# Second block: attention starts behind 7 projection steps, compressed branches last

## The chip, the cores and the metric

The kernel runs on one core of a Trainium2 chip, as one program. The metric is the device time of one execution in microseconds. TensorE (PE) does the matmuls, VectorE (DVE) and ScalarE (ACT) the elementwise work and everything that leaves PSUM, GpSimd (POOL) next to nothing here, and SyncE (SP) issues the loads. The engines run side by side; each works off its own list of instructions in order and waits on semaphores (counters) that the others raise.

## What is computed

A block of two layers (a mixture of experts among its parts) is followed by a second block of two layers, all in float32, on one sequence of 256 tokens of width 1024. The change is in the second block, in the part from the input projection to the mixers:

```python
for l in range(DEPTH):                                   # DEPTH = 2
    h = rms_norm_2(x, ln1_gain[l])
    proj = h @ w_in[l]                                   # 1024 x 2866, split into:
    (nsa_q, k_cmp, v_cmp, k_slc, v_slc, k_win, v_win, nsa_gate,
     mla_cq, mla_ckv, mla_kpe, ret_q, ret_k, ret_v, ret_gate) = jnp.split(proj, offsets, axis=-1)
    o_nsa = nsa_mixer(partial_rope(nsa_q), partial_rope(k_cmp), v_cmp, ...)   # 6 heads, 3 branches each
    o_mla = mla_mixer(mla_cq, mla_ckv, mla_kpe, ...)                          # 5 heads
    o_ret = retention_mixer(ret_q, ret_k, ret_v, ret_gate, ...)               # 5 heads
    x = x + jnp.concatenate([o_nsa, o_mla, o_ret], axis=-1) @ w_out[l]
    h = rms_norm_2(x, ln2_gain[l])
    x = x + jnp.square(jax.nn.relu(h @ w_up[l])) @ w_down[l]

# nsa_mixer, per head: gate0 * softmax(q @ kc) @ vc + gate1 * softmax(q @ k_slc) @ v_slc + gate2 * softmax(q @ k_win) @ v_win
# with kc = gelu(blocks(k_cmp) @ w1_k) @ w2_k, and vc likewise (15 compressed positions)
# mla_mixer: q and k come from the normalised latents: rms(c_q) @ w_uq, rms(c_kv) @ w_ukv, ropes on 32 of 96 dims
# retention_mixer: group norm of the retained values, times silu(ret_gate)
```

The selected and the window branch are both plain causal attention at this length. The three branches of a head are summed, so their order is free.

## The kernel before

One layer of the second block runs `block2_pe`, `block2_act` and `block2_dve` side by side, each engine its own function. The work between the norm and the retention is cut into *steps* and *units*, whose order is written out by hand in three tables and the list of branches.

**Steps.** `STEPS` is one list; a step is a projection (`p nq0`: 8 matmuls of 128 by 256 into a bank of `acc`, which ScalarE copies out), a rope (`r nq0`: one matmul that turns the halves, then three VectorE instructions, lines 930, 932, 935), a matmul from the latents (`m mq0`, `m mk0`, `m mv0`, line 3006, copied out by ScalarE in line 3027) or `sums` (the two sums of squares of the latents, lines 2923 to 2925). `p kpe` takes rq0 along and `p rk0` takes rg0. The steps alternate between two banks of PSUM: step n waits until what step n-2 left there is read (`step_read`), by ScalarE's copy for p and m, by VectorE's rope for r. `STEPS_FIRST` holds the 19 steps ahead of the attention; between them stand, in banks of their own, the three parts of the compression network: `cmp_hidden_pe` (line 2883), `cmp_join_pe` (line 2890, with GELU on ScalarE in 2867) and `cmp_out_pe` (lines 2898 and 2900).

**Units.** A unit u is one branch of one head. `att_pe`, `att_act` and `att_dve` go through units in pairs. On TensorE: the steps beside u (`BESIDE[u]`), at even u the scores of the next pair (line 1018) and the values of the last pair (lines 1048 to 1053), then the transposes ("turn") of unit u's probabilities (line 1028 for compressed, 1031 for the others). On VectorE: mask and maximum of unit u+1 (lines 1080, 1084), normalisation of unit u (1091 to 1104), at odd u the finished heads' outputs (line 1125), then the steps beside u. On ScalarE: exponentials of unit u+1 (line 1133), copies of the steps beside u (line 909 for projections), copy of the turned probabilities of u ("probT", line 1146 or 1148).

The units of before: for each of three head pairs the compressed, the selected and the window branch (units 0 to 17), then the five heads of the latent attention (units 18 to 22). Steps stand beside units 0 to 17; none stands beside the latent heads.

**ScalarE's tables.** A function of another table set needs a table load first. The exponential, the sigmoid of the gates (part of the nvw projections), GELU, the square root and the Silu of the gates rg0 to rg2 (applied when the projection is copied out) are such functions; copies and squares need none.

**Loads.** SP issues the loads in the order of the list `AFTER`, into a ring of 7 slots: the load of item n waits until the slot of item n-7 is freed, by the last matmul that reads it.

## Time and profile before

| | us |
|---|---|
| median of 3 runs | 2389.46 |
| lowest and highest run | 2384.75, 2391.63 |
| profiled execution: own time, its span | 2383.3 |
| attention part, layer 0 and layer 1 (norm's end to first retention scores) | 151.1, 149.6 |

The profiled execution has no time beside its span; what lies around it is not shown. A row of the timeline gives the start, the length and, in brackets, how long the engine was idle ahead of it and what ended that. Every float32 matmul stands as two passes, so 8 matmuls read x16.

### The profile page before, as it was taken

Reading aid. Unit: us, or ns where it says so; the run is one execution under the profiler, and the core shown is the slowest. Engines: PE = TensorE matmul, PEld = TensorE weight load, DVE = VectorE, ACT = ScalarE, POOL = GpSimd, SP = SyncE. Lnnn points to the kernel's source line nnn. Section 1 sums busy time; section 2 is a strip of 40 time slices with the busy share of each in tenths; the row PEclk is TensorE's granted clock in tenths of the full one; section 3 lists DMA queues with packets and bytes.
Section 4 is the critical chain, followed back from the end, with each engine's and each line's share of the span. In section 5 each row is a group of like instructions: output and inputs, shape, how many; then the busy total and the mean of one; then the engine's idle time right before and its main releaser. Section 6 shows DMA issues by size and latency. Waiting matters only on the chain.

```text
span 2383.3 us, 36172 instructions
## 1 busy us (share of the span) xinstructions
PE 2273.9 (95%) x15501; PEld 1593.8 (67%) x15502; DVE 916.8 (38%) x2168; ACT 391.0 (16%) x903; POOL 27.9 (1%) x52
## 2 busy tenths in 40 slices
PE   7989999998999999998999999889899999989999
PEld 5758998876763444434444444366589998659999
DVE  3664887448420000000000010034656733457763
ACT  3222100022320000000000000014520002451101
POOL 1010000000100000000000000000000000000000
PEclk8998999998899999999999999999999999999999
DMA  9471478933169999999989999982225463323541
GB/s 358 166 252 36 159 248 310 384 114 107 36 247 378 369 409 411 409 413 407 384 305 364 408 410 410 411 285 103 71 80 169 177 194 126 123 71 107 176 157 41
DMA packets 240082, 582.97 MB, mean 245 GB/s; under 512 B 22170, under 2 KB 106658, under 8 KB 227636
## 3 DMA queue, kind: packets, MB, share of 16 engines
q1 hardware_dynamic: 239348, 580.52, 65.6%
q8 instruction: 124, 2.03, 0.3%
q14 instruction: 34, 0.28, 0.0%
q0 software_dynamic: 576, 0.13, 0.0%
HBM read 579.58 MB, written 1.05 MB: 244 GB/s over the span
## 4 chain that ended last, share of the span: by engine, by line
PE 83%; DMA 6%; DVE 5%; SPq 2%; ACT 2%; issue 1%; DVEq 0%; ACTq 0%
PE wrk L2486 13%; PE acc L876 8%; PE acc L2546 5%; PE acc L3272 5%; PE acc L3304 5%; PE wrk L2471 4%; PE wrk L3304 4%; PE wrk L3272 4%; PE acc L1658 3%; DMA ring<-in_moe_w_down_dram 3%; PE acc L879 3%; PE wrk L2493 3%; PE wrk L1658 3%; PE acc L953 2%; PE acc L2529 2%; PE acc L968 2%
## 5 line engine op out<-in xcount | busy, mean ns | idle before, releaser
L2486 PE MATMUL wrk<-ring,hT 128*64 128x512 f32 (+1 forms) x1792 | 348.1, 542 | 6.7 <-DMA ring<-in_moe_w_up_dram 3.4
L2730 DVE TENSOR_TENSOR scratch<-scratch,wrk 128x512 f32<-128x512 f32 (+4 forms) x32 | 24.5, 767 | 802.3 <-PE wrk L2486 594.9
L2486 PEld LDWEIGHTS wrk<-ring,hT 128*64 128x64 f32 x1792 | 126.2, 137 | 203.9 <-issue 186.9
L876 PE MATMUL acc<-hT,ring 128*128 128x256 f32 x1024 | 232.5, 384 | 1.3 <-ACT scratch L909 0.5
L876 PEld LDWEIGHTS acc<-hT,ring 128*128 128x128 f32 x1024 | 194.0, 192 | 29.9 <-issue 1.9
L2546 PE MATMUL acc<-ring,scratch 128*64 128x512 f32 x784 | 177.7, 597 | 14.9 <-DMA ring<-in_moe_w_down_dram 14.9
L3349 DVE TENSOR_TENSOR ring<-ring 128x512 f32<-128x512 f32 (+1 forms) x192 | 155.2, 862 | 1.2
L2546 PEld LDWEIGHTS acc<-ring,scratch 128*64 128x64 f32 x784 | 54.0, 136 | 116.9 <-issue 102.2
L3304 PE MATMUL acc<-scratch,ring 128*128 128x128 f32 x1024 | 117.6, 275 | 0.0
L3304 PEld LDWEIGHTS acc<-scratch,ring 128*128 128x128 f32 x1024 | 116.0, 192 | 0.0
L2665 ACT ACTIVATE scratch<-wrk 128x512 f32<-128x512 f32 (+4 forms) x32 | 21.1, 661 | 527.2 <-PE wrk L2518 527.2
L2471 PE MATMUL wrk<-ring,hT 128*128 128x512 f32 x224 | 96.9, 593 | 0.0
L879 PE MATMUL acc<-ring,hT 128*128 128x384 f32 (+5 forms) x384 | 82.6, 372 | 10.4 <-ACT scratch L909 6.2
L3304 PE MATMUL wrk<-scratch,ring 128*128 128x128 f32 x768 | 89.0, 275 | 0.0
L3272 PE MATMUL acc<-mixT,ring 128*128 128x128 f32 x768 | 88.4, 275 | 0.0
L3304 PEld LDWEIGHTS wrk<-scratch,ring 128*128 128x128 f32 x768 | 87.4, 192 | 0.0
L3272 PEld LDWEIGHTS acc<-mixT,ring 128*128 128x128 f32 x768 | 87.0, 192 | 0.0
L909 ACT ACTIVATE scratch<-acc 128x256 f32<-128x256 f32 (+8 forms) x118 | 41.3, 360 | 259.5 <-PE acc L876 166.6
L879 PEld LDWEIGHTS acc<-ring,hT 128*128 128x128 f32 x384 | 61.1, 197 | 30.8 <-issue 7.3
L1678 PE MATMUL acc<-scratch,ring 128*128 128x256 f32 x352 | 78.7, 386 | 2.5 <-DMA ring<-in_ffn_w_down_dram 1.8
L2493 PE MATMUL wrk<-ring,hT 128*32 128x256 f32 (+1 forms) x1536 | 77.6, 354 | 0.0
L2471 PEld LDWEIGHTS wrk<-ring,hT 128*128 128x128 f32 x224 | 42.3, 190 | 52.5 <-issue 52.5
(459 smaller groups left out, 3002.9 us busy)
## 6 DMA issues: line engine op xcount, KB each, us to landing
ring<-in_moe_w_gate_dram SPq DMA_DIRECT2D x56, 2048.0 KB, 20.3
ring<-in_moe_w_up_dram SPq DMA_DIRECT2D x56, 2048.0 KB, 20.7
ring<-in_moe_w_down_dram SPq DMA_DIRECT2D x56, 2048.0 KB, 18.9
ring<-in_w_ada_dram SPq DMA_DIRECT2D x24, 2048.0 KB, 17.5
ring<-in_w_up_dram SPq DMA_DIRECT2D x32, 1024.0 KB, 6.6
ring<-in_w_down_dram SPq DMA_DIRECT2D x32, 1024.0 KB, 6.6
ring<-in_w_out_dram SPq DMA_DIRECT2D x8, 2048.0 KB, 9.0
ring<-in_w_in_dram SPq DMA_DIRECT2D x8, 1536.0 KB, 15.9
```

The lines of the kernel that those rows point to most:

```text
L876: mm = pe.matmul(acc[p0:p0 + m, bank, 0:S], cols(k), hT[:, k, :], start=(k == 0), stop=(k == KD - 1))
L879: mm = pe.matmul(acc[:, bank, 0:m], hT[:, k, t], cols(k), start=(k == 0), stop=(k == KD - 1))
L953: pe.matmul(accv[:, 4 * h + m, :], w[:, k, m * P:(m + 1) * P], mixT[:, k, :], start=(k == ks[0] and m % 2 == 0), stop=False, skip_group_ch ...
L1658: mm = pe.matmul(PRODUCT[x][:, t * P:(t + 1) * P], stationary[x][:, k, t * P:(t + 1) * P], moving[x][:, k, :], start=(k == 0), stop=(k == ...
L1678: mm = pe.matmul(accv[:, m, :], w[:, j, m * P:(m + 1) * P], DENSE_TILES[:, 4 * g + j, :], start=(g == 0 and j == 0 and m % 2 == 0), stop=( ...
L2471: mm = pe.matmul(flat_wrk[:, lo + c * 512:lo + (c + 1) * 512], hT[:, k, 0:P], w[:, at_, c * 512:(c + 1) * 512], start=(k == 0), stop=(k == ...
L2486: mm = pe.matmul(flat_wrk[h * HD:h * HD + HD, lo:lo + n2], hT[:, k, 0:HD], w[:, at_, h * n2:(h + 1) * n2], start=(k == 0), stop=(k == KD - ...
L2493: mm = pe.matmul(flat_wrk[quarter(c), lo + n2:lo + n2 + n4], hT[:, k, LIGHT:MIDDLE], w[:, at_, c * n4:(c + 1) * n4], start=(k == 0 and n2 ...
L2546: mm = pe.matmul(acc[h * HD:h * HD + HD, 0, :], turned[:, at_:at_ + HD], w[:, j, h * 512:(h + 1) * 512], start=(g == 0 and n == 0), stop=( ...
L3272: mm = pe.matmul(up_region(x)[:, t * P:(t + 1) * P], stationary[x][:, k, t * P:(t + 1) * P], moving[x][:, k, :], start=(k == 0), stop=(k = ...
L3304: mm = pe.matmul(PRODUCT[x][:, m * P:(m + 1) * P], stationary[x][:, t, m, :], moving[x][:, t, :], start=(i == 0 and t == 0 and m == 0), st ...
L3349: ins = dve.tensor_tensor(part(out_), part(a), part(b), ALU.subtract)
```

## The change

The order of steps and units is rewritten. Ahead of the attention stand 7 steps: nq0, nks, nvw0, rope nq0, nvw1, rope nks, nq1. The units run: selected branches of head pairs 0 and 1 (units 0 to 3), their window branches (4 to 7), selected and window branches of pair 2 (8 to 11), the compressed branches of all three pairs (12 to 17), then the latent heads (18 to 22). Steps stand beside units 0 to 21: beside 7 `c join` and kpe, beside 8 `c out`, rope kpe and `sums`, beside 9 rq1, beside 10 rq2 and rope rq0, beside 11 mq0 and rk1, beside 12 mq1, mq2 and rope rq1, beside 13 rk2, rope mq0 and mq3, beside 14 mq4, rope mq1, mk0 and mk1, beside 15 rope mq2, mk2, mk3 and rope rq2, beside 16 ropes mq3 and mq4, mk4, mv0 and mv1, beside 17 to 21 rk0, rv0, rv1, rg1 and rg2 with the ropes of rk1, rk2 and rk0 between. The compression network's three parts become steps (`c parts`, `c join`, `c out`) in the alternating banks, beside units 6, 7 and 8. Their intermediate tensors, the latent keys and the latent values get other places, since their old ones are in use then. The Silu of the gates moves from the copy of the projections to the start of the retention (`ret_act`). Each unit waits for its own inputs and no longer for those of the last. The load of the latents' weights moves ahead of three of the projection's. Heads of pair 2 share banks with those of pair 0, in other columns.

```diff
     for layer in range(DEPTH):
-        after += [("in2", layer, i) for i in range(3)] + [("cmp", layer)]
-        after += [("in2", layer, i) for i in range(3, len(IN2))] + [("mla", layer), ("decay", layer)] + [("out2", layer, h) for h in range(2)]
+        after += [("in2", layer, i) for i in range(3)] + [("cmp", layer), ("in2", layer, 3), ("mla", layer)]
+        after += [("in2", layer, i) for i in range(4, len(IN2))] + [("decay", layer)] + [("out2", layer, h) for h in range(2)]
         n = D_FF // 512
         for kind in ("sup", "sdown"):
...
@@ -1005,6 +1005,10 @@
 
             return ((0, 15), (16, 31)) if kind == "cmp" else ((0, P), (P, 384))
 
+        def head_sum(b):
+
+            return acc[b["p0"]:b["p0"] + HD, b["head"] % 2, b["col"]:b["col"] + S]
+
         def att_scores_pe(pe, tag, pair, branches):
             for u in pair:
                 for s, v in branches[u]["ready"]:
...
             plan += rk[1:] + rk[:1]
-            plan += rows("rv", 5, 0, 320, t_v) + heads5("rg", 6, 0, t_g, ACT.Silu)
+            plan += rows("rv", 5, 0, 320, t_v) + heads5("rg", 6, 0, t_g)
             return plan
 
         def rope2(l):
...
-        def cmp_gelu_act(act, l):
+        def cmp_parts_act(act, l, bank):
+            act.wait_ge(freed_by_pe, freeing(("cmp", l)))
+            act.activation(n_part, acc[:, bank, 0:2 * P].rearrange("p (a h) -> p a h", a=2), ACT.Copy)\
+               .then_inc(act_done, up("act", "hidden parts", l))
+
+        def cmp_gelu_act(act, l, bank):
             act.wait_ge(pe_done, at("pe", "hidden", l))
-            act.activation(n_hid[:, :, 0:30], wrk[:, 3, 0:64].rearrange("p (a n) -> p a n", a=2)[:, :, 0:30], ACT.Gelu_apprx_tanh)\
+            act.activation(n_hid[:, :, 0:30], acc[:, bank, 0:64].rearrange("p (a n) -> p a n", a=2)[:, :, 0:30], ACT.Gelu_apprx_tanh)\
                .then_inc(act_done, up("act", "hidden", l))
 
-        def cmp_act(act, l):
-            act.wait_ge(freed_by_pe, freeing(("cmp", l)))
-            act.activation(n_kcT[:, 0:15], wrk[:, 1, 0:15], ACT.Copy).then_inc(act_done, up("act"))
-            act.activation(n_vcT[0:15, :], wrk[0:15, 2, 0:P], ACT.Copy).then_inc(act_done, up("act", "compressed", l))
-
-        def cmp_hidden_pe(pe, l):
+        def cmp_act(act, l, bank):
+            act.wait_ge(pe_done, at("pe", "compressed", l))
...
-                act.activation(l_k[64:96, h, :], l_kpe[64:96, 0, :], ACT.Copy).then_inc(act_done, up("act", "kpe", l) if h == 4 else up("act"))
-
-
-
-
-        STEPS_FIRST = ("p nq0", "p nq1", "p nq2", "p nkc", "p nvc", "p nks", "r nkc", "p nvs0", "p nvs1", "r nks", "p nkw",
-                       "r nq0", "p nvw0", "r nq1", "p nvw1", "r nkw", "r nq2", "p cq0", "p cq1")
-        BESIDE = (("p ckv", "p kpe"), ("p rq1", "sums"), ("p rq2", "r kpe"), ("p rk1", "r rq0"), ("p rk2", "r rq1"),
-                  ("p rk0", "r rq2"), ("p rv0", "r rk1"), ("p rv1", "r rk0"), ("p rg1", "r rk2"), ("p rg2", "m mq0"),
-                  ("m mq1", "m mq2"), ("r mq0", "m mq3"), ("r mq1", "m mq4"), ("r mq2", "m mk0"), ("r mq3", "m mk1"),
-                  ("r mq4", "m mk2"), ("m mk3", "m mk4"), ("m mv0", "m mv1"))
...
+        BESIDE = (("r nq1", "p nkw"), ("r nkw", "p nvs0"), ("p nvs1", "p nkc"), ("r nkc", "p nq2"), ("r nq2", "p nvc"),
...
@@ -2978,6 +2989,8 @@
                 return act_done, at("act", "proj", ("2", l), BESIDE_IT.get(name, name))
             if kind == "m":
                 return act_done, at("act", "mla", l, name)
+            if kind == "c":
+                return act_done, at("act", {"parts": "hidden parts", "join": "hidden", "out": "compressed"}[name], l)
             if kind == "sums":
                 return dve_done, at("dve", "latent mean squares", l)
             return dve_done, at("dve", "rope", rope_step(l, name)[0], name)
...
             out = []
-            for i, br, g_ in [(i, br, g_) for i in range(3) for br in range(3) for g_ in range(2)]:
+            order = [(i, br) for half in ((0, 1), (2,)) for br in (1, 2) for i in half] + [(i, 0) for i in range(3)]
+            for i, br, g_ in [(i, br, g_) for i, br in order for g_ in range(2)]:
                 h, kind = 3 * g_ + i, ("cmp", "slc", "win")[br]
                 rows = slice(HD * g_, HD * g_ + HD)
...
                 out.append(dict(q=q, k=k, v=v, mask=K("cmp_hide") if br == 0 else K("causal"), kind="cmp" if br == 0 else "causal",
-                                scale=float(HD) ** -0.5, gate=lambda t, c=3 * h + br: n_gate[:, t, c:c + 1], first=br == 0,
-                                last=br == 2, head=2 * i + g_, p0=HD * (h % 2), place=mixT[HD * (h % 2):HD * (h % 2) + HD, h // 2, :],
-                                ready=[(act_done, at("act", "compressed", l)),
-                                       (dve_done, at("dve", "rope", ("2", l), "nq2"))] if (h, br) == (0, 0) else [],
+                                scale=float(HD) ** -0.5, gate=lambda t, c=3 * h + br: n_gate[:, t, c:c + 1], opens=br == 1 and i < 2,
+                                last=br == 0, head=2 * i + g_, p0=HD * (h % 2), col=S * (i // 2), over=[],
+                                place=mixT[HD * (h % 2):HD * (h % 2) + HD, h // 2, :],
+                                ready=[(act_done, at("act", "compressed", l)), (dve_done, at("dve", "rope", ("2", l), f"nq{i}")),
+                                       (dve_done, at("dve", "rope", ("2", l), ("nks", "nks", "nkw")[br]))][0 if br == 0 else 1:3 if br else 1],
+                                v_ready=[(act_done, at("act", "proj", ("2", l), ("nvs1", "nvs1", "nvw1")[br]))] if br else [],
                                 mask_ready=[]))
             for h in range(5):
                 p0 = HD * (h % 2)
-                out.append(dict(q=l_q[0:96, h, :], k=l_k[0:96, h, :], v=lambda t, h=h: l_v[:, t, HD * h:HD * h + HD],
-                                mask=K("causal"), kind="causal", scale=96.0 ** -0.5, gate=None, first=True, last=True, p0=p0, head=6 + h,
+                out.append(dict(q=l_q[0:96, h, :], k=l_k[h][0:96, :], v=lambda t, h=h: l_v[:, t, HD * h:HD * h + HD],
+                                mask=K("causal"), kind="causal", scale=96.0 ** -0.5, gate=None, opens=True, last=True, p0=p0, head=6 + h,
+                                col=0, over=((0, 4), (1, 5), (6,), (7,), (8,))[h],
                                 place=mixT[p0:p0 + HD, 3 + h // 2, :], mask_ready=[],
-                                ready=[(act_done, at("act", "mla", l, "mk4")), (dve_done, at("dve", "rope", ("mla", l), "mq4"))] if h == 0 else [],
+                                ready=[(act_done, at("act", "mla", l, f"mk{h}")), (dve_done, at("dve", "rope", ("mla", l), f"mq{h}"))],
                                 v_ready=[(act_done, at("act", "mla", l, "mv1"))] if h == 0 else []))
             return out
...
@@ -3130,6 +3151,9 @@
             outproj_first_pe(pe, items[1], 1, (0, 1), ATTENDED2)
 
         def ret_act(act, l):
+            act.wait_ge(act_done, at("act", "proj", ("2", l), "rg2"))
+            act.activation(t_g[UPPER, 0, :], t_g[UPPER, 0, :], ACT.Silu).then_inc(act_done, up("act"))
+            act.activation(t_g[:, 1:3, :], t_g[:, 1:3, :], ACT.Silu).then_inc(act_done, up("act", "ret gates", l))
             act.wait_ge(pe_done, at("pe", "ret out", l, 4))
             act.activation(t_q[UPPER, 0, :], acc[UPPER, 0, 0:S], ACT.Copy).then_inc(act_done, up("act"))
             act.activation(t_q[:, 1:3, :], acc[:, 1:3, 0:S], ACT.Copy).then_inc(act_done, up("act", "ret o", l))
...
 
-        LATENTS_AT, SHARED_KEY_AT = 0, 11
-        assert STEPS[-1] == "m mv1" and "p rg2" in STEPS[:steps_beside(SHARED_KEY_AT)[0]]
+        VALUE_BLOCKS_AT, KEY_BLOCKS_AT = 4, 3
+        LATENTS_AT, SHARED_KEY_AT = 7, 9
 
         def block2_pe(pe, l):
...
                 step_dve(dve, l, n)
-                if STEPS[n] == "r nkc":
-                    value_blocks_dve(dve, l)
-                if STEPS[n] == "r nkw":
-                    key_blocks_dve(dve, l)
 
             def beside(u):
                 if u == LATENTS_AT + 3:
                     latents_dve(dve, l)
                 for n in steps_beside(u):
                     step_dve(dve, l, n)
+                if u == VALUE_BLOCKS_AT:
+                    value_blocks_dve(dve, l)
+                if u == KEY_BLOCKS_AT + 2:
+                    key_blocks_dve(dve, l)
 
             att_dve(dve, tag, branches2(l), beside)
             ret_dve(dve, l)
```

What the order of the built program shows at three places, the names being as in the lines above.

ScalarE around the step that waits for the copies of the compressed keys and values. Before, the two copies (15 columns) stand ahead of the first unit:

```order
L2867 ACTIVATE scratch<-wrk 128x2x30
L909 ACTIVATE scratch<-acc 128x256
L2872 ACTIVATE scratch<-wrk 128x15
L2873 ACTIVATE scratch<-wrk 15x128
L1133 ACT_TABLE_LOAD
L1133 ACTIVATE scratch,stat<-scratch,stat 128x15 x4
L909 ACTIVATE scratch<-acc 128x256
L909 ACTIVATE scratch<-acc 32x256
L909 ACTIVATE scratch<-acc 64x256
L2929 ACTIVATE scratch<-scratch 128x512
```

After, they stand behind the squares of the latents (2939, 2940), a probT (1152), a load and the exponentials of unit 9:

```order
L2873 ACT_TABLE_LOAD
L2873 ACTIVATE scratch<-acc 128x2x30
L909 ACTIVATE scratch<-acc 32x256
L909 ACTIVATE scratch<-acc 64x256
L2939 ACTIVATE scratch<-scratch 128x512
L2940 ACTIVATE scratch<-scratch 128x256
L1152 ACTIVATE scratch<-wrk 128x384
L1137 ACT_TABLE_LOAD
L1137 ACTIVATE scratch,stat<-scratch,stat 128x128
L1137 ACTIVATE scratch,stat<-scratch,stat 128x256
L2878 ACTIVATE scratch<-acc 128x15
L2879 ACTIVATE scratch<-acc 15x128
```

So the copies (2878, 2879) moved behind two table loads, GELU's and the exponential's, and a unit; on TensorE the step `sums` (2933) follows two steps behind them.

TensorE in the latent steps (3006 before and 3021 after are latent matmuls, 921 ropes). Before, one rope stands in each unit:

```order
L921 MATMUL acc<-scratch,const 96x256
L3006 MATMUL acc<-scratch,ring 64x256
L1028 MATMUL wrk<-const,scratch 15x128 x2
L921 MATMUL acc<-scratch,const 96x256
L3006 MATMUL acc<-scratch,ring 64x256
L1018 MATMUL wrk<-scratch 128x128 x2
L1018 MATMUL wrk<-scratch 128x256 x2
L1048 MATMUL acc<-scratch 64x256 x2
L1031 MATMUL wrk<-const,scratch 128x128 x3
L921 MATMUL acc<-scratch,const 96x256
L3006 MATMUL acc<-scratch,ring 64x256
```

After, units 14 to 16 carry two ropes and two to three latent matmuls with hardly anything between:

```order
L921 MATMUL acc<-scratch,const 96x256
L3021 MATMUL acc<-scratch,ring 64x256 x2
L1022 MATMUL wrk<-scratch 128x15 x4
L1052 MATMUL acc<-scratch 64x256 x2
L1032 MATMUL wrk<-const,scratch 15x128 x2
L921 MATMUL acc<-scratch,const 96x256
L3021 MATMUL acc<-scratch,ring 64x256 x2
L921 MATMUL acc<-scratch,const 128x256
L1032 MATMUL wrk<-const,scratch 15x128 x2
L921 MATMUL acc<-scratch,const 96x256 x2
L3021 MATMUL acc<-scratch,ring 64x256
L3021 MATMUL acc<-ring,scratch 128x320 x2
```

What moved is that the latent matmuls and their ropes stand beside six units instead of nine, all of compressed branches.

TensorE in the latent heads. Before, only scores, values and turns are there:

```order
L1018 MATMUL wrk<-hT,scratch 128x128 x2
L1018 MATMUL wrk<-hT,scratch 128x256 x2
L1031 MATMUL wrk<-const,scratch 128x128 x3
L1018 MATMUL wrk<-hT,scratch 128x128 x2
L1018 MATMUL wrk<-hT,scratch 128x256 x2
L1051 MATMUL acc<-scratch 64x256 x2
L1053 MATMUL acc<-scratch 64x128 x2
L1031 MATMUL wrk<-const,scratch 128x128 x6
```

After, projections (876, 879) and the last ropes stand between them:

```order
L1022 MATMUL wrk<-table,scratch 128x128 x2
L1022 MATMUL wrk<-table,scratch 128x256 x2
L1052 MATMUL acc<-scratch 64x256 x2
L1035 MATMUL wrk<-const,scratch 128x128 x3
L879 MATMUL acc<-ring,hT 128x320 x8
L921 MATMUL acc<-scratch,const 128x256
L1035 MATMUL wrk<-const,scratch 128x128 x3
L876 MATMUL acc<-hT,ring 128x256 x8
L921 MATMUL acc<-scratch,const 64x256
L1022 MATMUL wrk<-mixT,scratch 128x128
L1022 MATMUL wrk<-mixT,scratch 128x256
L1055 MATMUL acc<-scratch 64x256 x2
```

The retention's own projections moved here from beside units 5 to 9.

## Rows read from the trace of the kernel before

**Rows 1.** The page: the chain that ended last, share of the span by engine.
```profile
PE 83%; DMA 6%; DVE 5%; SPq 2%; ACT 2%; issue 1%; DVEq 0%; ACTq 0%
```

**Rows 2.** Busy time by stretch: length; PE, PEld, DVE, ACT, POOL; granted clock; DMA.
```profile
1600.00:1628.40 28.40, 25.02 (x201) 20.84 (x200) 10.01 (x28) 9.13 (x25) 0.00 (x0) 1.00 0.10 32
1628.40:1700.00 71.60, 70.30 (x380) 47.40 (x380) 36.56 (x169) 36.84 (x98) 0.00 (x0) 1.00 0.38 132
1700.00:1713.40 13.40, 10.39 (x63) 5.76 (x62) 10.82 (x49) 8.18 (x32) 0.00 (x0) 1.00 0.01 2
1713.40:1730.30 16.90, 11.63 (x67) 7.60 (x66) 10.74 (x50) 7.71 (x28) 0.00 (x0) 0.90 0.00 0
2099.60:2113.00 13.40, 10.26 (x63) 5.63 (x62) 10.92 (x49) 8.29 (x32) 0.00 (x0) 1.00 0.01 2
2113.00:2128.40 15.40, 10.25 (x68) 6.73 (x67) 10.58 (x50) 7.71 (x28) 0.00 (x0) 1.00 0.00 1
```

**Rows 3.** Timeline of TensorE in the head: start, length, operation, idle before.
```profile
1611.19 0.59 PE L921 MATMUL acc<-scratch,const 128*128 128x256 f32 x2
1613.61 2.25 PE L879 MATMUL acc<-ring,hT 128*128 128x146 f32 x16 [1.82 <-ACT scratch L909]
```

**Rows 4.** Timeline of ScalarE at the same place.
```profile
1612.07 1.28 ACT L909 ACT_TABLE_LOAD   x1
```

**Rows 5.** Timeline of TensorE: pair kpe+rq0; a projection to the next projection.
```profile
1632.60 9.07 PE L892 MATMUL acc<-hT,ring 128*32 128x256 f32 x32
...
1658.07 3.62 PE L876 MATMUL acc<-hT,ring 128*128 128x256 f32 x16
...
1663.89 0.44 PE L892 MATMUL acc<-hT,ring 128*64 128x256 f32 x2
```

**Rows 6.** Timeline of ScalarE: squares of the latents; probT, table load, two exponentials.
```profile
1642.11 0.63 ACT L2929 ACTIVATE scratch<-scratch 128x512 f32<-128x512 f32 x1
1642.64 0.40 ACT L2930 ACTIVATE scratch<-scratch 128x256 f32<-128x256 f32 x1
...
1653.77 0.49 ACT L1148 ACTIVATE scratch<-wrk 128x384 f32<-128x384 f32 x1
1654.28 1.28 ACT L1133 ACT_TABLE_LOAD   x1
...
1656.37 0.18 ACT L1133 ACTIVATION_READ_ACCUMULATOR scratch<-scratch,stat 128x1 f32 x1
```

**Rows 7.** Timeline of VectorE: latents; mask, normalisation, rope of a compressed unit; head outputs; rope's add.
```profile
1654.30 3.35 DVE L796 RECIPROCAL scratch<-scratch 128x512 f32<-128x512 f32 x1
...
1658.47 0.48 DVE L2944 SCALAR_TENSOR_TENSOR scratch<-scratch,vec 128x256 f32<-128x256 f32 x1
...
1697.46 0.16 DVE L1080 CUSTOM_DVE_ANT_0 scratch<-wrk,const 128x15 f32<-128x15 f32 x1
...
1697.84 0.17 DVE L1091 CUSTOM_DVE_ANT_0 scratch<-scratch,const 128x15 f32<-128x15 f32 x1
...
1699.14 0.42 DVE L930 TENSOR_TENSOR scratch<-scratch,table 96x256 f32<-96x256 f32 x1
...
1700.27 0.28 DVE L1080 CUSTOM_DVE_ANT_0 scratch<-wrk,const 128x128 f32<-128x128 f32 x1
...
1702.24 0.88 DVE L1125 COPY mixT<-acc 64x256 f32<-64x256 f32 x2
...
1704.01 0.42 DVE L935 TENSOR_TENSOR scratch<-scratch 96x256 f32<-96x256 f32 x1
```

**Rows 8.** Timeline of TensorE behind that add.
```profile
1704.58 0.64 PE L921 MATMUL acc<-scratch,const 96*96 96x256 f32 x2 [1.84 <-DVE scratch L935]
```

**Rows 9.** Timeline of TensorE: last turn, last values, first retention scores.
```profile
1727.71 0.55 PE L1031 MATMUL wrk<-const,scratch 128*128 128x128 f32 x3
1728.84 0.65 PE L1051 MATMUL acc<-scratch,hT 128*64 128x256 f32 x2 [0.58 <-ACT scratch L1148]
...
1730.31 0.71 PE L3090 MATMUL wrk<-scratch 64*128 64x256 f32 x4 [0.60 <-DVE mixT L1125]
```

84 lines of the change are left out of this document (43 added, 41 removed), and 5 rows, old and new, of the table BESIDE.

## The prediction

> **What bounds the kernel now.** I read the chain of work that ended last first: 83% of the span is TensorE, 6% transfers, 5% VectorE [rows 1]. So only TensorE's own instructions and the holes between them count. Then I cut the attention part of each layer of the second block, from 1600 us on (before that it is projections without a hole), into four stretches and read the busy time of each engine [rows 2]. In layer 0 TensorE stands idle 28.40 - 25.02 = 3.4 us in the first (the *head*, up to the first unit's scores), 71.60 - 70.30 = 1.3 in the second (the *middle*, units 0 to 12, most with a projection beside them), 13.40 - 10.39 = 3.0 in the third (the *latent steps*, where small matmuls and ropes alternate) and 16.90 - 11.63 = 5.3 in the fourth (the *tail*, the five latent heads with nothing beside them): 13.0 us. Layer 1 reads the same (3.1 and 5.2 in the last two), except that its tail is 15.40 us long and not 16.90: in layer 0 the granted clock is 0.90 there, between the levels 2.4 and 1.2 GHz, and that cost 1.5 us. Transfers are no bound here: the DMA share in these stretches is 0.38 at most [rows 2]. In SP's queue the load of the latents' weights moves ahead of those of rk, rv and rg. Those of rv and rg now wait for nq2 (unit 3) and nvc (unit 4) to be read and are used beside units 18 to 21, a good 50 us later; the first load of the MLP waits for mv1 (unit 16) and is used after the retention.
>
> The change issues the same matmuls in another order, so no TensorE work goes away. It can gain at most these 13 us a layer and the 1.5. The question is only where holes close and where new ones open. All that follows is counted as the profile counts idle: from the modelled end of a matmul.
>
> **Head.** The hole before the second nvw projection is a ScalarE table load: nvw0 ends at 1611.19, nvw1 starts at 1613.61 with 1.82 us idle [rows 3], and the load stands between the two evictions [rows 4]. After the change, ScalarE comes to that eviction free (the copy of the blocks no longer stands ahead of it), but load and gate column still lie on the path: from the load's start to nvw1's start 1613.61 - 1612.07 = 1.54, plus the first copy and its handover, about 0.4, less the rope matmul in between, 0.6. That leaves 1.35. The holes ahead of the compression network (0.9) and of the first scores (0.4) go with the move, and so does the rest of the 3.4. A tenth comes with nq1's rope. Head after: 1.4; gain 2.0.
>
> **Middle.** Two new waits. First, `sums` is the second step behind `c out`, so it takes its bank and waits until ScalarE has copied the compressed keys and values. Those copies stand behind a whole unit: squares, probT of unit 7, and, since GELU changed the table, a load, the exponentials of unit 9, then the copies. The pair kpe+rq0 ends at 1641.60 in the trace [rows 5]; squares start 0.5 behind that and, 0.63 and 0.40 long but overlapped, let the next instruction start at about +1.35. From a probT's start through the load to the end of two exponentials it is 1656.55 - 1653.77 = 2.78 [rows 6]; the two small copies and the handover add 0.5. So `sums` may start at 4.6. TensorE's own work up to it (turn, c out, rope of kpe) is 1.75. Hole: 2.9, as the profile counts 2.75. Second, the latents: after rq1, ScalarE copies it, loads the root's table and takes the root, 2.5; VectorE's reciprocal and three products take 1658.95 - 1654.30 = 4.65 [rows 7]; with handovers the latents are ready 7.4 behind rq1. TensorE has until then one turn, 0.4, and the sequence projection, rope, compressed scores, values, turn, which takes 1663.89 - 1658.07 = 5.8 [rows 5]. Hole before mq0: 1.2, and then 0.4 before rk1, which waits for rq0's rope, queued behind the latents. Against this stand the loads of Silu's table, which go from the units (the middle's 1.3 is one of them). Small waits of this kind elsewhere: 0.0 to 0.4, taken 0.1. Middle after: 2.75 + 1.1 + 0.35 = 4.2; loss 2.9.
>
> The Trainium skill (ScalarE: Activation LUTs, "What ACT_TABLE_LOAD costs") puts 1.38 us of drain on top of the load's 1.28 at each switch. The trace does not agree: the load of 1654.28 begins 0.02 behind the probT ahead of it, and no gap of that length follows it [rows 6]. By the page the hole before `sums` would be 1.4 larger; I take the rows.
>
> **Latent steps.** In units 14 to 16 every second step's bank waits for a rope. VectorE's prices [rows 7]: masking a compressed unit 0.38, normalising it 1.30, a rope 1.13 (1699.14 to 1700.27), two head outputs 0.98, and TensorE goes on 0.57 behind the start of a rope's last add (1704.01 there, 1704.58 in [rows 8]). From the start of projection rk2 at 0: r mq0 at 3.5, its rope's add at 4.55, so mq4 goes at 5.2. VectorE then masks 15, normalises 14 and ropes mq1, add at 7.4: mk1 goes at 8.0, where TensorE was ready at 7.1 (0.9). Scores of 16 end at 9.0; VectorE stood idle for them 1.3, then masks 16, normalises 15, copies two outputs and ropes mq2, add at 12.4: mk3 goes at 13.0, ready at 10.7 (2.3). The rope of rq2 is behind it: r mq4 waits 0.5. Then mask 17, normalise 16, ropes of mq3 and mq4: mk4 goes at 18.0, ready at 15.5 (2.4), mv0 at 19.3 (0.9). With 0.25 for two copies on ScalarE it is 7.2, seven holes, and the profile counts 0.16 less of each: 6.1 against 3.1. Loss 3.0. Before, each unit had one rope; after, units 15 and 16 have two, and one has head outputs besides.
>
> **Tail.** Five projection steps of 3.5 to 4.4 us now stand beside units 17 to 21, where VectorE needs 4.1 at most a unit. The holes of 1.3, 0.3, 1.0, 0.3 and 1.2 go. What stays is the chain of the last units: turn, copy, values from 1727.71 to 1728.84, of which 0.58 is a hole, now twice since nothing is beside unit 22, and 0.60 for the last head output [rows 9]. Tail after: 1.75; gain 3.45. The retention's Silu (a load and two instructions, about 2.3 us of ScalarE) runs while TensorE computes the retention scores and values, some 5 us; without that cover it would cost those 2.3.
>
> **Sum.** Per layer -2.0 + 2.9 + 3.0 - 3.45 = +0.45, twice +0.9. The tail's clock loss of layer 0 goes with its holes, -1.5. Together -0.6 on the profiled span, 2383.3, which is 6.2 below the median of the runs, 2389.46. I forecast 2388.9: no difference that can be measured (0.3%, 7.2 us, is about what a measurement of this kernel can tell).
>
> **Rivals.** *The new holes do not open* (chance 0.30). If ScalarE and VectorE run further ahead than I have them, `sums` finds its bank read and the ropes cost no more than today. For it: in the middle both engines are busy half of the time only (36.6 and 36.8 of 71.6). Against it: the order of the instructions on both, which leaves no way around those waits. Then 2.75 and 3.0 fall out of each layer: 2388.9 - 11.5 = 2377.4. *TensorE's clock* (chance 0.18, slower). After the change, units 14 to 16 hold TensorE idle 6 of 20 us. In layer 0's tail, a stretch with a third idle, the clock was granted at 0.90; in layer 1's, equally idle, at 1.00 [rows 2], so it is not certain. The price is decided by what runs when the clock is low: before it was small work for heads, after it is the pair rk0+rg0 and rv0, 8 us at 2.4 GHz, that follow at once. If 8 us of it and 3 of the latent steps run at 1.2 GHz in both layers, that adds 11 us a layer less what was waiting anyway (6): +5 each, and the -1.5 does not come: 2388.9 + 10 + 1.5 = 2400.4. From 3 us a layer on, it is slower. The Trainium skill (TensorE: Matmul & The Clock Gate) lets the clock follow TensorE's activity; layer 0 and 1 differing under equal work shows that here the phase decides too. *The change is not what it says* (0.02): the order of the built program shows the attention's first scores behind 7 steps; excluded but for a wait on a transfer, with in_w_in's two last loads now later in the queue.
>
> **Chances and range.** The forecast, 0.50, has its own range 2382 to 2396. Low end 2374: the rival's 2377.4 with the head's hole gone as well. High end 2400. Faster by over 0.3% 0.30, within 0.3% 0.52, slower 0.18.
>
> **What would show it.** In the profile after: the idle before L2933 (`sums`) is ACT's, 2.5 to 3 us in each layer; a step L3021 waits 2 us or more for DVE L935 twice a layer; the tail from unit 17 on has TensorE idle under 2.5; ScalarE has 6 table loads a layer from the first projection to the last unit instead of 11, and one more in the retention. I am wrong if the wait before L2933 is under 1 us or the latent steps lose under 4: then it is the first rival. If all holes are as said and the stretch is still longer, the clock row of units 14 to 18 must be under 0.9.

## The result

The changed kernel takes 2398.81 us (median of 12 executions, 2391.72 to 2403.87), the kernel before, beside it, 2387.68 (12 executions, 2376.45 to 2396.41). The ratio is 1.0041 [1.0025, 1.0056], which is 9.8 us; the medians differ by 11.1. It is slower by 0.4%. The forecast was 2388.9 and no measurable difference. The range from 2374 to 2400.4 holds the time; the direction was not foreseen.

### The profile page after: what moved, and what is told of

Read it like the earlier page. It is cut to its first block, busy times and chain, and to the rows that moved or that the text cites. A ratio compares the mean times of both kernels' runs of the same rounds, so it can differ in the third digit from the quotient of the medians.

```text
span 2396.1 us, 36216 instructions
## 1 busy us (share of the span) xinstructions
PE 2285.1 (95%) x15501; PEld 1599.0 (67%) x15502; DVE 917.0 (38%) x2168; ACT 383.6 (16%) x899; POOL 28.0 (1%) x52
## 4 chain that ended last, share of the span: by engine, by line
PE 84%; DVE 5%; DMA 5%; ACT 3%; SPq 2%; issue 1%; DVEq 0%; ACTq 0%
PE wrk L2490 13%; PE acc L876 8%; PE acc L2550 5%; PE acc L3297 5%; PE acc L3329 5%; PE wrk L2475 4%; PE wrk L3329 4%; PE wrk L3297 4%; PE acc L879 3%; PE acc L1662 3%; DMA ring<-in_moe_w_down_dram 3%; PE wrk L2497 3%; PE wrk L1662 3%; PE acc L953 2%; PE acc L2533 2%; PE acc L968 2%
## 5 line engine op out<-in xcount | busy, mean ns | idle before, releaser
L2669 ACT ACTIVATE scratch<-wrk 128x512 f32<-128x512 f32 (+4 forms) x32 | 21.1, 661 | 527.2 <-PE wrk L2522 527.2
L909 ACT ACTIVATE scratch<-acc 128x256 f32<-128x256 f32 (+7 forms) x118 | 41.3, 361 | 261.7 <-PE acc L876 177.1
```

## The profile after

First the stretches of TensorE in the changed kernel, layer 0 and then two of layer 1, in the columns of [rows 2] (stretch and length, busy us of the five engines, granted clock, DMA share, GB/s):

```profile
1576.20:1590.00 13.80, 12.35 (x69) 10.72 (x70) 9.32 (x21) 2.87 (x7) 0.00 (x0) 1.00 0.97 339
1603.00:1649.00 46.00, 43.88 (x292) 30.61 (x292) 17.04 (x76) 19.22 (x57) 0.00 (x0) 1.00 0.36 125
1649.00:1656.00 7.00, 6.13 (x30) 4.27 (x31) 2.76 (x13) 1.52 (x9) 0.00 (x0) 0.76 0.01 2
1656.00:1684.00 28.00, 25.95 (x146) 19.23 (x144) 15.96 (x69) 14.45 (x47) 0.00 (x0) 1.00 0.22 76
1684.00:1708.00 24.00, 19.03 (x78) 9.90 (x77) 11.79 (x57) 6.07 (x23) 0.00 (x0) 0.72 0.28 88
1708.00:1734.15 26.15, 24.17 (x119) 17.53 (x120) 12.14 (x50) 9.55 (x28) 0.00 (x0) 1.00 0.26 81
...
2055.00:2062.00 7.00, 5.67 (x28) 3.99 (x29) 2.30 (x11) 1.52 (x7) 0.00 (x0) 0.76 0.01 4
...
2091.00:2115.00 24.00, 19.58 (x76) 10.21 (x75) 11.84 (x54) 6.40 (x23) 0.00 (x0) 0.64 0.29 88
```

In both attention parts the clock is granted in full everywhere but in two places of each layer: around `sums` (0.76) and around units 14 to 16 (0.72 and 0.64). Now each attention part whole, from the norm's end to the first retention scores, in the same columns, the changed kernel and then the one before:

```profile
1576.17:1734.15 157.98, 144.11 (x803) 102.44 (x804) 76.22 (x312) 59.27 (x183) 0.00 (x0) 0.95 0.32 106
1982.67:2140.67 158.00, 144.71 (x803) 102.66 (x804) 71.30 (x303) 59.28 (x183) 0.00 (x0) 0.94 0.24 81
...
1579.21:1730.31 151.10, 138.13 (x804) 99.92 (x804) 76.09 (x312) 63.78 (x186) 0.00 (x0) 0.99 0.34 115
1978.82:2128.42 149.60, 136.61 (x803) 98.94 (x804) 71.13 (x303) 63.87 (x186) 0.00 (x0) 1.00 0.25 83
```

Both parts are 158.0 long, 6.9 and 8.4 more than before (151.1 and 149.6). TensorE idles 13.87 and 13.29 of it, where it was 12.97 and 12.99: **the holes cost +1.2 us in both layers together** (forecast +0.9). **TensorE's busy time rose by 6.0 and 8.1 us**, with the same matmuls. That is half-speed work, as the rows below show. (The profiled span rose by 12.8 and not by 15.3, mainly since the first part started 3.0 us earlier; nothing that the change touches lies ahead of it. In the profiled executions of all the kernels below that start lies anywhere between 1573.8 and 1587.6.)

The waits of TensorE (engine, line, waited for: us in total, times, longest) show the two big causes:

```profile
PE acc L3021 <- DVE scratch L935: 10.0, 8, 2.2
PE acc L2933 <- ACT scratch L2879: 5.7, 2, 2.8
```

TensorE's timeline at the first of them, and ScalarE's ahead of it (start, length, line, operation, count, idle time before it and its releaser):

```profile
1646.41 0.61 PE L921 MATMUL acc<-scratch,const 32*32 32x256 f32 x2
1649.87 0.85 PE L2933 MATMUL acc<-scratch,const 128*128 128x256 f32 x2 [2.84 <-ACT scratch L2879]
1650.51 1.06 PE L2934 MATMUL acc<-scratch,const 128*128 128x256 f32 x2
1651.36 1.06 PE L2935 MATMUL acc<-scratch,const 128*128 128x256 f32 x2
1652.35 1.54 PE L1022 MATMUL wrk<-scratch 64*128 64x128 f32 x8
```

```profile
1647.22 1.28 ACT L1137 ACT_TABLE_LOAD   x1
1648.52 0.40 ACT L1137 ACTIVATE scratch<-scratch,stat 128x128 f32<-128x128 f32 x1
...
1648.92 0.49 ACT L1137 ACTIVATE scratch<-scratch,stat 128x256 f32<-128x256 f32 x1
...
1649.47 0.25 ACT L2879 ACTIVATE scratch<-acc 15x128 f32<-15x128 f32 x1
```

The hole is the forecast one: `sums` waits 2.84 us for copies that stand behind the exponential's table load. Behind it a pass pair of 128x256 takes 1.06 instead of 0.59, and the unit's scores 1.54 instead of 0.93 (the times at full clock are f_both's, below). The second place:

```profile
1688.05 1.08 PE L3021 MATMUL acc<-scratch,ring 128*64 128x256 f32 x2 [2.07 <-DVE scratch L935]
1689.07 1.22 PE L921 MATMUL acc<-scratch,const 128*128 128x256 f32 x2
...
1690.51 1.49 PE L921 MATMUL acc<-scratch,const 96*96 96x256 f32 x4
1694.16 0.66 PE L3021 MATMUL acc<-scratch,ring 128*64 128x256 f32 x2 [2.16 <-DVE scratch L935]
1695.48 2.47 PE L3021 MATMUL acc<-ring,scratch 128*128 128x320 f32 x4 [0.66 <-DVE scratch L935]
1697.74 2.77 PE L1022 MATMUL wrk<-scratch 96*128 96x128 f32 x8
...
1702.02 5.04 PE L892 MATMUL acc<-hT,ring 128*64 128x256 f32 x32
```

Again the holes before mk3 (2.07) and mk4 (2.16) are those of the forecast, and again what follows runs at half speed: the latent values 2.47 (1.31 at 2.4 GHz, see f_both below), the scores 2.77 (1.47), the pair rk0+rg0 5.04 (3.67).

## Experiments: is it the clock or the holes?

Theory A: the holes let TensorE's clock fall from 2.4 to 1.2 GHz, and the slow work behind them is the price. Theory B: the holes themselves are. Four kernels fill the holes with matmuls whose result nobody reads, without shortening a wait:

```diff
+        def fill_pe(pe, l, u, n):
+            if n:
+                pe.wait_ge(act_done, at("act", "probT", ("2", l), u - 2))
+            for _ in range(n):
+                pe.matmul(wrk[:, 2 + u % 2, 384:512], ones, K("slot_ids")[:, 0:P], start=True, stop=True, skip_group_check=True)
+
         def step_pe(pe, l, n):
             kind, _, name = STEPS[n].partition(" ")
+            fill_pe(pe, l, *{'sums': (8, 10), 'm mk3': (15, 7), 'm mk4': (16, 7), 'm mv0': (16, 2)}.get(STEPS[n], (2, 0)))
```

This is f_both; each entry is a step with its unit and the number of unread matmuls ahead of it. f_sums has the first entry alone, f_lat the other three, f_half 5, 3 and 3 at the first three. Lines behind the helper stand 7 further down (L3021 is L3028).

**f_sums.** 

> The changed kernel with 10 matmuls of 128 columns that nobody reads (about 0.27 us each, 2.7 together) in TensorE's queue ahead of the latents' sums, into the unused columns of a PSUM bank. Waits and order stay as they were, so the hole of 2.84 us before L2933 is filled and nothing else changes. Theory A (the clock): the sums and the scores behind them ran at half speed because TensorE stood idle ahead of them; filled, they run at 2.4 GHz. Extra time of the half-speed stretch, from the rows: three sums at 1.06 instead of 0.53 and two score pairs, about 2 us a layer, so 4 us less than the changed kernel: about 2394.5 beside its 2398.8, and the granted clock of the 7 us around it 1.00 instead of 0.76. Theory B (the holes themselves are the price): 0 to +1, 2398.8 to 2400.

**f_lat.** 

> The changed kernel with unread matmuls of 128 columns in the three largest holes of the latent steps only: 7 before mk3, 7 before mk4, 2 before mv0 (1.9, 1.9 and 0.5 us). Theory A (the clock): the stretch of 24 us around units 14 to 16 has a granted clock of 0.72 and 0.64 in the two layers; at 1.00 it gives back most of the added busy time, which is 5.9 and 8.1 us in the two layers less 2 for the sums: 4 and 6, so about 10 us less: 2389. Part may be lost again, since mk4 waits for VectorE and comes no earlier: 2389 to 2393. Theory B (the holes, clock without effect): 2398 to 2400.

**f_both.** 

> Both sets of unread matmuls. Theory A (the clock): the two gains add up, 12 to 14 us less than the changed kernel: 2385 to 2388, which is level with the kernel before, as the sum of the holes said (+1.2 by the rows of the two layers). The mean granted clock is over 0.98 instead of 0.975. Theory B: 2398 to 2401, since filling a hole doesn't shorten a wait.

All results stand in one table. "Parts" is the length of the two attention parts in the profiled execution, "idle" TensorE's in both together. "Lost" is (1 - mean granted clock of all executions) times the median: at most so much would a full clock have saved, over the whole program. Each ratio is to the kernel before as measured beside that run (medians 2385.67 to 2389.79; the row shown stands beside f_sums, f_lat, f_both and sums7).

| kernel | median us | ratio to before | parts us | idle us | lost us |
|---|---|---|---|---|---|
| before (35 executions) | 2387.78 | | 151.1, 149.6 | 26.0 | 51.5 |
| changed | 2398.81 | 1.0041 [1.0025, 1.0056] | 158.0, 158.0 | 27.2 | 61.0 |
| changed, again | 2397.25 | 1.0034 [1.0019, 1.0049] | 156.1, 158.2 | 27.0 | 59.7 |
| f_sums | 2391.07 | 1.0012 [1.0000, 1.0025] | 154.1, 154.5 | 21.6 | 52.4 |
| f_lat | 2389.25 | 1.0004 [0.9990, 1.0019] | 152.5, 154.0 | 21.1 | 48.2 |
| f_both | 2385.31 | 0.9991 [0.9977, 1.0005] | 150.9, 151.2 | 16.2 | 44.7 |
| f_half | 2392.23 | 1.0013 [1.0001, 1.0026] | 150.9, 151.2 | 23.3 | 50.2 |
| silu_back | 2399.09 | 1.0035 [1.0017, 1.0053] | 159.3, 156.7 | 29.7 | 59.7 |
| sums7 | 2388.95 | 1.0000 [0.9986, 1.0014] | 149.1, 150.5 | 18.9 | 59.5 |
| sums7_fill | 2380.32 | 0.9952 [0.9935, 0.9970] | 146.7, 147.1 | 13.8 | 46.2 |
| spread | 2373.66 | 0.9946 [0.9927, 0.9964] | 145.6, 147.2 | 18.0 | 45.1 |
| spread2 | 2384.48 | 0.9982 [0.9970, 0.9994] | 147.7, 147.7 | 20.5 | 50.7 |
| best | 2378.97 | 0.9964 [0.9945, 0.9983] | 149.0, 147.7 | 17.3 | 48.8 |
| best2 | 2375.69 | 0.9939 [0.9918, 0.9961] | 144.2, 144.1 | 13.4 | 46.3 |

f_both does more work on TensorE than the changed kernel, in the same order with the same waits, and is 13.5 us faster (11.9 by the two ratios). Its stretches and its timeline at the same two places:

```profile
1573.79:1724.69 150.90, 142.95 (x856) 104.87 (x856) 76.21 (x312) 59.35 (x183) 0.00 (x0) 1.00 0.35 116
1973.20:2124.42 151.22, 142.95 (x855) 104.86 (x856) 71.32 (x303) 59.32 (x183) 0.00 (x0) 1.00 0.25 83
```

```profile
1647.48 0.67 PE L2933 MATMUL acc<-scratch,const 128*128 128x256 f32 x2 [0.41 <-ACT scratch L2879]
1647.99 0.59 PE L2934 MATMUL acc<-scratch,const 128*128 128x256 f32 x2
...
1648.95 0.93 PE L1022 MATMUL wrk<-scratch 64*128 64x128 f32 x8
...
1684.03 0.62 PE L3028 MATMUL acc<-scratch,ring 128*64 128x256 f32 x2 [0.31 <-DVE scratch L935]
...
1690.48 1.31 PE L3028 MATMUL acc<-ring,scratch 128*128 128x320 f32 x4
1691.63 1.47 PE L1022 MATMUL wrk<-scratch 96*128 96x128 f32 x8
...
1693.93 3.67 PE L892 MATMUL acc<-hT,ring 128*64 128x256 f32 x32
```

Theory B said 2398 to 2401 for it: it has fallen. f_both lies in A's 2385 to 2388, f_lat in A's 2389 to 2393, and f_sums gained more (7.7) than A's 4. In f_sums' trace a part of that lies where nothing was filled: from mk3 to the end of the pair rk0+rg0 TensorE took 15.7 and 16.0 us instead of 19.0, while mq0 and rk1 took longer than there (last section). So how much work runs slow behind an unfilled hole differs between executions, and the gains of the two fillings do not add up (7.7 and 9.6, together 13.5).

The lost column agrees for whole executions: the changed kernel lost 9.5 us more to the clock than before, and idles 1.2 more: 10.7, against 11.1 between the medians.

**The change again, and one part undone.** 

> The changed kernel itself once more, beside the three others on this chip. All theories: 2397 to 2400, both attention parts 158.0 us long with TensorE idle 13 to 14 and a granted clock of 0.94 to 0.95. If the slower clock were chance, the two layers would not come out alike again.

It repeats, but for the part of layer 0: 156.1 instead of the 158.0 expected; there the pair rk0+rg0 ran at full speed. In the next kernel the Silu is at the copies again:

```diff
-            plan += rows("rv", 5, 0, 320, t_v) + heads5("rg", 6, 0, t_g)
+            plan += rows("rv", 5, 0, 320, t_v) + heads5("rg", 6, 0, t_g, ACT.Silu)
...
-            act.wait_ge(act_done, at("act", "proj", ("2", l), "rg2"))
-            act.activation(t_g[UPPER, 0, :], t_g[UPPER, 0, :], ACT.Silu).then_inc(act_done, up("act"))
-            act.activation(t_g[:, 1:3, :], t_g[:, 1:3, :], ACT.Silu).then_inc(act_done, up("act", "ret gates", l))
...
-            dve.wait_ge(act_done, at("act", "ret gates", l))
```

> The changed kernel with one part undone: Silu stands at the eviction of rg0, rg1 and rg2 again, as before the change, and not in the retention. ScalarE then loads Silu's table and the exponential's again in three units of the tail, 2.6 us each time, in units of some 4 us in which it is busy 2. If TensorE does not wait for ScalarE there: 2398 to 2400, no difference. If it does, up to 1.3 a unit and layer: to 2406.

TensorE waits for it at rv0, in both layers:

```profile
1715.94 4.54 PE L879 MATMUL acc<-ring,hT 128*128 128x320 f32 x16 [1.40 <-ACT scratch L909]
```

and the last values wait 1.38 instead of 0.78: idle time 29.7 against 27.0 in the repeated kernel. The medians, 2399.09 and 2397.25, cannot tell the two apart. By the idle time of these two traces, moving the Silu gained about 1.3 us a layer; it is not what made the change slow.

**How small must a hole be?** 

> f_both with about half of the unread matmuls: 5 of 10 ahead of the sums, 3 of 7 ahead of mk3 and of mk4, none before mv0. About 1.5 us of hole stay at the sums and about 1.3 before mk3 and mk4. The hole of 1.43 before the second nvw projection and that of 1.06 before mq0 mostly had no slow matmuls behind them. If it is the large hole that lets the clock fall, the small ones leave it at 2.4 GHz: 2385 to 2387 as f_both, both attention parts about 151. If the clock follows the sum of idle time over a stretch, about half of the loss comes back: 2390 to 2393, parts of 153 to 155.

```profile
1651.67 0.67 PE L2933 MATMUL acc<-scratch,const 128*128 128x256 f32 x2 [1.53 <-ACT scratch L2879]
1652.18 0.59 PE L2934 MATMUL acc<-scratch,const 128*128 128x256 f32 x2
...
1693.35 0.62 PE L3028 MATMUL acc<-scratch,ring 128*64 128x256 f32 x2 [1.50 <-DVE scratch L935]
```

Inconclusive. In the profiled execution nothing behind the holes of 1.53, 1.20 and 1.50 is slow, and the parts are as long as f_both's. But that execution (2384.57) is the fastest of 12; the median is 6.9 above f_both's, and the lost column 5.5. So in most executions the clock probably falls somewhere all the same; where, the one trace doesn't show.

## Experiments: the holes closed by the order

sums7 takes the wait of `sums` away by where it stands:

```diff
-                  ("p cq0", "p cq1"), ("c parts", "p ckv"), ("c join", "p kpe"), ("c out", "r kpe", "sums"), ("p rq1",),
+                  ("p cq0", "p cq1"), ("c parts", "p ckv"), ("sums", "c join", "p kpe"), ("c out", "r kpe"), ("p rq1",),
...
-        LATENTS_AT, SHARED_KEY_AT = 7, 9
+        LATENTS_AT, SHARED_KEY_AT = 6, 9
```

> The changed kernel with the latents' squares at unit 6 and the sums ahead of the join of the compression network, at unit 7 (root and latents a unit earlier too). The sums' bank is then read by a copy that stands two units back, so the hole of 2.84 before L2933 goes, and the latents are ready before mq0, so its 1.06 goes too. Theory A (clock): 3.9 of holes plus 2 of half speed a layer, 11 to 12 us less than the changed kernel: 2387, with the latent steps' stretch still at 0.6 to 0.7. Theory B (holes only): 7.8 less, 2391. If the wait is only passed on to the compression's output (which waits for GELU), under 3 less: 2396 to 2399.

```profile
1647.29 0.60 PE L2933 MATMUL acc<-scratch,const 128*128 128x256 f32 x2
...
1649.69 9.04 PE L892 MATMUL acc<-hT,ring 128*32 128x256 f32 x32 [0.58 <-DVE scratch L2945]
```

The hole of 2.84 is gone and 0.58 stands in its place, mq0's 1.06 is gone too: 8.3 us less idle time than the changed kernel. The median, 2388.95, lies between A's 2387 and B's 2391 and decides nothing. It is level with before although it idles 7.1 us less, because the latent steps still lose to the clock (lost column 59.5 against 51.5; TensorE busy 139.8 and 140.8 in the two parts against the 136.6 of before's layer 1, where the clock never fell). With these filled:

> sums7 (the latents' sums a unit earlier) with unread matmuls in the three holes of the latent steps as in f_lat. Theory A (clock): sums7 has TensorE busy 139.8 and 140.8 us in the two attention parts and a granted clock of 0.79 around units 14 to 16; before had 136.6 where the clock never fell, so 3.2 and 4.2 are half speed. Filled, they go: 145.9 and 146.3 us a part, 7.4 less than sums7, 2381 to 2382. Theory B (holes): 2389 as sums7, since the filling shortens no wait.

The parts are 146.7 and 147.1, 0.8 longer than A's 145.9 and 146.3, and the median is 2380.3. B, which said 2389, is excluded: no execution was above 2383.9. The interval of its ratio lies below 1. Next the latent steps were spread, so that projections close their holes (the lines are against sums7; the load of the latents' weights also goes behind that of rk, in the list `AFTER`):

```diff
-        after += [("in2", layer, i) for i in range(3)] + [("cmp", layer), ("in2", layer, 3), ("mla", layer)]
-        after += [("in2", layer, i) for i in range(4, len(IN2))] + [("decay", layer)] + [("out2", layer, h) for h in range(2)]
+        after += [("in2", layer, i) for i in range(3)] + [("cmp", layer), ("in2", layer, 3), ("in2", layer, 4), ("mla", layer)]
+        after += [("in2", layer, i) for i in range(5, len(IN2))] + [("decay", layer)] + [("out2", layer, h) for h in range(2)]
...
-                  ("p rq2", "r rq0"), ("m mq0", "p rk1"), ("m mq1", "m mq2", "r rq1"), ("p rk2", "r mq0", "m mq3"),
-                  ("m mq4", "r mq1", "m mk0", "m mk1"), ("r mq2", "m mk2", "m mk3", "r rq2"),
-                  ("r mq3", "r mq4", "m mk4", "m mv0", "m mv1"), ("p rk0", "r rk1"), ("p rv0",), ("p rv1", "r rk2"),
+                  ("r rq0", "p rq2", "m mq0"), ("r mq0", "p rk1", "m mq1"), ("m mk0", "r mq1", "m mk1"),
+                  ("m mq2", "p rk2", "r rq1"), ("m mk2", "r mq2", "m mq3"), ("m mk3", "p rk0", "r mq3"),
+                  ("m mq4", "r rq2", "m mk4"), ("m mv0", "r mq4", "m mv1"), ("p rv0", "r rk1"), ("p rv1", "r rk2"),
```

> sums7 with the twelve latent steps spread over units 10 to 17 between the projections rq2, rk1, rk2 and rk0+rg0, never more than one rope a unit, and no step two places behind a rope unless a projection or a unit's own work stands between (the load of the latents' weights goes behind that of rk). Both theories: the holes of 2.1 and 1.7 before mk3 and mk4 go, about 3 to 4 us a layer. Theory A adds the half-speed time, 3.2 and 4.2: in all 13 to 15 us less than sums7, 2374 to 2376, with a granted clock of 1.00 in both attention parts. Theory B: 6 to 8 less, 2381 to 2383. If VectorE is what units 12 to 17 really wait for, the holes only move: over 2384.

2373.66, as A said, and like sums7_fill clearly faster than the kernel before. A's clock of 1.00 in both parts did not quite come: layer 1 has 0.99, and there the pair rk0+rg0 ran slow behind a hole of only 0.73, which the same place in layer 0 (0.74) did not show:

```profile
2072.04 1.07 PE L3021 MATMUL acc<-scratch,ring 128*96 128x256 f32 x4 [0.73 <-DVE scratch L1108]
...
2075.20 4.99 PE L892 MATMUL acc<-hT,ring 128*64 128x256 f32 x31
```

Two refinements (spread2: order latent step, rope, projection within each unit, beginning with mq0 at unit 10; best: also nvw0 ahead of nks):

> spread with the steps of a unit in the order latent step, rope, projection, so that the step two places behind a rope is never a short one that finds the rope unfinished. In spread, mq0 waits 1.09 us for rope rq0 and mq2 0.74, mk4 0.70, mv 0.77. With a projection of 3.7 us between, mq0's wait should go, mq2's is behind a compressed unit's turn and may stay: 1 to 1.5 us less a layer, so 2 to 3 less than spread: 2371, attention parts 144 and 145. If VectorE's chain in units 12 to 17 sets the pace (its masking, normalising and rope take 2.8 of 3.3 us), the waits only move: 2373 to 2375.

> spread2 with the second and third projection exchanged (nvw0 ahead of nks): a projection of 3.7 us then runs while ScalarE loads Sigmoid's table between the two copies of nvw0, so the hole of 1.43 before nvw1 goes in both layers: 2.9 less than spread2, 2368. In layer 0 the third part of the weights is needed 3.7 us earlier, where the DMA share is 0.97; if it lands after 1578, TensorE waits there for the transfer instead, and layer 0 gains nothing: 2370.

Both missed. One mistake is in the traces of both: leading unit 10, mq0 waits for the latents themselves (line 2954) and no longer for a rope. spread2 first, then best:

```profile
1663.29 1.10 PE L3021 MATMUL acc<-scratch,ring 128*96 128x256 f32 x4 [2.59 <-DVE scratch L2954]
...
1665.33 3.72 PE L876 MATMUL acc<-hT,ring 128*128 128x256 f32 x16 [0.36 <-ACT scratch L3042]
```

```profile
1661.39 2.02 PE L3021 MATMUL acc<-scratch,ring 128*96 128x256 f32 x4 [2.59 <-DVE scratch L2954]
...
1664.38 5.46 PE L876 MATMUL acc<-hT,ring 128*128 128x256 f32 x16
```

The same hole of 2.59 is followed by full speed in the one and by half speed in the other (5.46 instead of 3.72), in layer 1 likewise (3.72 and 5.18). That hole does not explain all of spread2's miss: its parts are 2.5 us longer than spread's together, its median is 10.8 higher (8.6 by the ratios), and its lost column 5.6. As in f_half, other executions probably lose what the traced one does not; no trace shows where. The exchange of nvw0 and nks did close the 1.43 in both layers. The last kernel moves mq0 to unit 11 (lines against spread, the load order being spread's):

```diff
+        STEPS_FIRST = ("p nq0", "p nvw0", "p nks", "r nq0", "p nvw1", "r nks", "p nq1")
...
+                  ("r rq0", "p rq2"), ("m mq0", "r rq1", "p rk1"), ("m mq1", "r mq0", "m mk0"),
+                  ("m mq2", "r mq1", "p rk2"), ("m mk1", "r mq2", "m mq3"), ("m mk2", "r mq3", "p rk0"),
+                  ("m mk3", "r rq2", "m mq4"), ("m mk4", "r mq4", "m mv0"), ("m mv1", "r rk1", "p rv0"),
+                  ("p rv1", "r rk2"), ("p rg1", "r rk0"), ("p rg2",))
```

> spread with three edits. The first latent step mq0 comes a unit later, at 11, behind rope rq0 and projection rq2: in spread2, where it led unit 10, it waited 2.59 us for VectorE's latents, and that hole put half-speed matmuls back into the part. The order latent step, rope, projection holds from unit 11 on. nvw0 stands ahead of nks, as in best, where the hole of 1.43 was gone in both layers and the weights had landed in time. Sum: spread2's idle time of 10.2 us a part less 2.6 and 1.4 is 6.2, with 136.6 busy at 2.4 GHz: parts of 143, two of them 15 us less than before's 300.7: 2388 - 15 = 2373. If the clock still falls at some smaller hole, 1.5 to 3 more a part: up to 2379. If VectorE is late at the new places, parts of 145 and more.

```profile
1581.84:1725.99 144.15, 137.43 (x804) 99.09 (x804) 76.31 (x312) 58.69 (x183) 0.00 (x0) 1.00 0.35 119
1974.51:2118.65 144.14, 137.43 (x803) 99.09 (x804) 71.39 (x303) 58.68 (x183) 0.00 (x0) 1.00 0.26 86
```

Parts of 144.1, the shortest of all, with a full clock; 143 was expected. The median is 2375.69 (2373 expected), the ratio 0.9939 [0.9918, 0.9961], which is 14.5 us; the medians of the two differ by 10.0, from few executions (6 and 11). Against spread the medians (2375.69 and 2373.66, measured at different times) say nothing; the intervals of the ratios overlap almost wholly.

## Why the prediction was wrong, point by point

- **The bound** held: TensorE is 84% of the chain, and what changed is its own time in the two attention parts.
- **Head**: the hole before nvw1 was 1.43 (1.35 forecast), and a wait of the second scores for a rope adds 0.44: 1.9 instead of 1.4.
- **Middle**: `sums` 2.84 by the profile's count (2.75), mq0 1.06 (1.1), ahead of rk1 0.33 (0.35). Right.
- **Latent steps**: mk3 2.07 (2.3), mk4 2.16 (2.4), mk1 0.39 (0.9), mv0 0.66 (0.9). In the stretch from 1684 to 1708 TensorE idles 4.97, a little under the 6.1 for units 14 to 16.
- **Tail**: 1.98 (1.75). Two turned copies and the last head output remain [rows 9], here again:

```profile
1730.76 0.65 PE L1055 MATMUL acc<-scratch 128*64 128x256 f32 x4 [0.78 <-ACT scratch L1152]
...
1732.69 0.65 PE L1055 MATMUL acc<-scratch 128*64 128x256 f32 x2 [0.58 <-ACT scratch L1152]
...
1734.15 0.71 PE L3111 MATMUL wrk<-scratch 64*128 64x256 f32 x4 [0.60 <-DVE mixT L1129]
```

- **The sum of the holes**, +0.9, was +1.2. (Two slips of 0.1 in the working, the small waits that are named and not added, and 18.0 - 15.5 read as 2.4, change nothing.) The price of the table load without a drain behind it was right as well: in ScalarE's rows above the exponential starts at 1648.52, 0.02 behind the load's end. The Trainium skill (ScalarE: Activation LUTs, "What ACT_TABLE_LOAD costs") has 1.38 us of drain there; the trace does not agree. ScalarE has the 6 table loads a layer that were forecast, and one in the retention, where it had 11.
- **The step that failed** is "The tail's clock loss of layer 0 goes with its holes, -1.5", the only term on the clock in the sum. It credited the holes that go and charged nothing for those that come, which are about twice as long. In its place stood +14.1 in the profiled pair (busy +6.0 and +8.1) and +9.5 by the mean clocks of all executions. So of the 11.7 us between the forecast change (-0.6) and the measured one (+11.1 by the medians) the clock makes 11.0 and the holes 0.3.
- **The rival** on the clock (2400.4) was the case, in both layers of both traced executions; the mean clock of each of the 24 executions of the changed kernel lies at 0.972 to 0.977, that of before's 35 at 0.973 to 0.983. It had the place right only in part. It counted 8 us of the pair and rv0 and 3 of the latent steps; the pair lost 1.4 and 1.1, rv0 nothing, while the latent steps and the scores behind them, and `sums`, which it left out, lost the rest. That its sum came so near is therefore partly luck. Its chance of 0.18 came from one stretch ([rows 2], layer 0's tail 0.90, layer 1's 1.00), whose largest hole was 1.28. The new holes were 2.84, 2.07 and 2.16. That difference in size was in the text, and was not used. That "the phase decides" is not shown here; what the traces show is that equal queues can end either way.
- **What would show it** had the right test: all holes as said, the stretch longer, the clock under 0.9 in units 14 to 18. It was 0.72 and 0.64. Of the signs one held by half: a wait of 2 us or more at line 3021 stands twice in layer 0 (2.07, 2.16), once in layer 1 (2.06, then 1.67).

## What to carry to other kernels

When a change moves holes about on a TensorE that is otherwise busy, price each new hole of over about 2 us twice: once as idle time, and once as the work behind it at half speed. Against the 136.6 us of TensorE at full clock this second price was 7.5 and 8.1 us a layer in the changed kernel, and 3.2 and 4.2 in sums7, where only the holes of the latent steps were left. Smaller holes are not always free either (f_half's median, the 0.73 in spread). A wait can be cheap to keep if something harmless runs in it: filling four of a layer, the three largest among them, gave back 13.5 us with no other edit. Better is here an order in which the step two places behind a slow reader is a long one; and before a step is moved ahead, all of its inputs are to be looked up, not only the wait that one wants to remove (mq0 in spread2).
